# A gated-delta-rule inverse on one core: quadrant products and predicated copies in place of masked blocks and subtractions

## The reference, cut to what matters

```python
decay = jnp.exp(jnp.where(incl, G[..., :, None] - G[..., None, :], -jnp.inf))
kb = k * beta[..., None]
L = jnp.where(strict, jnp.einsum('bhncd,bhnsd->bhncs', kb, k) * decay, 0.0)
sol = lax.linalg.triangular_solve(L + jnp.eye(CHUNK), rhs, left_side=True, lower=True)
```

## Time and profile before

| what | value |
|---|---|
| median of 3 runs | 2124.07 us (2120.09 to 2124.46) |
| profiled execution, its own time | 2125.45 us |
| its span | 2123.6 us |
| mean granted TensorE clock | 0.997 |
| TensorE busy | 2078.8 us (98%) |
| VectorE busy | 1498.3 us (71%) |
| ScalarE busy | 891.7 us (42%) |
| GpSimd busy | 178.1 us (8%) |

### The profile page before, as it was taken

The page is one execution under the profiler, slowest core; times in us unless marked ns, Lnnn a source line. Parts: engine busy times, 40 slices in busy tenths (PEclk is TensorE's granted clock), DMA queues, the critical chain, the costliest instruction groups (busy, mean ns, idle before and its releaser), DMA issues.

```text
span 2123.6 us, 35703 instructions
## 1 busy us (share of the span) xinstructions
PE 2078.8 (98%) x14417; PEld 1808.5 (85%) x14417; DVE 1498.3 (71%) x1949; ACT 891.7 (42%) x1174; POOL 178.1 (8%) x152
## 2 busy tenths in 40 slices
PE   8999999999999999999999999999999999999999
PEld 8988888798888798888798878887879998778998
DVE  6968754778745577754697685456688877588887
ACT  3244444334444423444323454445554334664332
POOL 6630000000000000000073300000100000100000
PEclk9999999999999999999999999999999999999999
DMA  8512665552656453655464046565325555414552
GB/s 248 179 42 80 202 195 181 176 183 97 198 179 196 161 179 120 201 195 180 147 188 142 3 149 218 184 190 156 103 68 191 178 188 167 139 50 164 194 178 100
DMA packets 267625, 333.81 MB, mean 157 GB/s; under 512 B 20562, under 2 KB 230613, under 8 KB 267493
## 3 DMA queue, kind: packets, MB, share of 16 engines
q1 hardware_dynamic: 267493, 331.93, 48.3%
HBM read 330.84 MB, written 1.05 MB: 156 GB/s over the span
## 4 chain that ended last, share of the span: by engine, by line
PE 84%; DVE 10%; ACT 3%; issue 2%; SPq 1%; DMA 0%; POOL 0%; DVEq 0%; ACTq 0%
PE bank L586 47%; PE bank L554 25%; DVE pj L2199 2%; PE bank L1065 2%; ACT stat L1590 1%; PE bank L827 1%; PE bank L921 1%; PE bank L991 1%; PE bank L1146 1%; DVE w_hi L2238 1%; PE bank L637 1%; DVE sq L2199 1%; DVE pj L2193 1%; DVE w_lo L2240 1%; DVE pj L2189 1%
## 5 line engine op out<-in xcount | busy, mean ns | idle before, releaser
L2240 DVE TENSOR_TENSOR w_lo<-ring,w_hi 128x2048 fp32r<-128x2048 f32 (+2 forms) x289 | 615.3, 2131 | 371.8 <-ACT w_hi L1635 369.4
L1635 ACT ACTIVATE w_hi<-ring 128x2048 fp32r<-128x2048 f32 (+1 forms) x220 | 418.9, 1905 | 469.0 <-PE bank L586 287.3
L586 PE MATMUL bank<-w_lo,xh 128*128 128x512 f32 x992 | 267.0, 392 | 0.0
L586 PE MATMUL bank<-w_hi,xl 128*128 128x512 f32 x896 | 240.8, 391 | 1.0 <-DVE xl L2189 0.7
L586 PE MATMUL bank<-w_hi,xh 128*128 128x512 f32 x896 | 241.1, 391 | 0.6 <-ACT xh L1590 0.6
L554 PE MATMUL bank<-xh,w_lo 128*128 128x256 f32 (+2 forms) x1832 | 241.7, 284 | 0.0
L554 PE MATMUL bank<-xh,w_hi 128*128 128x256 f32 x1752 | 234.6, 287 | 0.8 <-ACT xh L1590 0.7
L554 PEld LDWEIGHTS bank<-xh,w_lo 128*128 128x128 f32 (+2 forms) x1832 | 228.6, 191 | 1.0
L554 PE MATMUL bank<-xl,w_hi 128*128 128x256 f32 x1752 | 229.3, 284 | 0.0
L554 PEld LDWEIGHTS bank<-xh,w_hi 128*128 128x128 f32 x1752 | 220.2, 191 | 9.6 <-issue 6.7
L554 PEld LDWEIGHTS bank<-xl,w_hi 128*128 128x128 f32 x1752 | 218.0, 191 | 1.0 <-issue 0.7
(11 more groups left out here) (325 smaller groups left out, 2439.1 us busy)
## 6 DMA issues: line engine op xcount, KB each, us to landing
ring<-in_ffn_w_in_dram SPq DMA_DIRECT2D x264, 512.0 KB, 4.5
ring<-in_ffn_w_down_dram SPq DMA_DIRECT2D x88, 512.0 KB, 4.1
ring<-in_gdn_w_in_dram SPq DMA_DIRECT2D x64, 512.0 KB, 5.0
ring<-in_ffn_w_out_dram SPq DMA_DIRECT2D x44, 512.0 KB, 3.7
ring<-in_w_in_dram SPq DMA_DIRECT2D x40, 512.0 KB, 4.7
ring<-in_hgrn_w_in_dram SPq DMA_DIRECT2D x32, 512.0 KB, 4.5
ring<-in_gla_w_in_dram SPq DMA_DIRECT2D x24, 512.0 KB, 4.7
ring<-in_gdn_w_out_dram SPq DMA_DIRECT2D x16, 512.0 KB, 4.4
```

Of the source, the lines that this page charges most:

```text
L586: m = nc.tensor.matmul(bank[:, 0:width], xin[:, k0 + k, rows_of], w[:, k, c * width:(c + 1) * width], start=(first and step == 0 and k == ...
L1635: nc.scalar.activation(taken(high_part(u), u), taken(ring[:, u % RING, :], u), ACT.Copy).then_inc(*act_hi.tick())
L2240: v.tensor_tensor(w_lo[:, u % RING, 0:share], w[:, 0:share], high[:, 0:share], ALU.subtract).then_inc(*dve_lo.tick())
```

## The change

`crossed` names the two off-diagonal quadrants. The stationary matrix of the product is now a whole 128x128 tile per matrix, `lb`, that holds minus the two diagonal blocks of L, each in the other block's columns, and zero elsewhere. One product of 128x128 by 64 columns serves both blocks; it does so by putting each block's result in the other block's partitions. X and XT of a matrix therefore lie in opposite halves. L isn't masked for levels 1 to 4; what must not change is left out when the result is put in place, by a predicated copy through a level mask instead of a subtraction. For level 5 GpSimd masks `lb` once. The order of the TensorE instructions changes to product of group n, correction of group n-2. The masks need a transposed form, made once in layer 0 by four transpositions and two copies.

```diff
-        lb_masked, lb = (flat(ct)[:, ...] for n in range(2))
+        crossed = ((blocks[0], blocks[1]), (blocks[1], blocks[0]))
+        lb = ct
...
+                    if layer == 0 and n == N_CONV - 2:
+                        masks_transposed()
...
+            def masks_transposed():
+                b = psum.claim(pe, "level masks")
+                pe.wait_ge(*pool_setup.at("constants"))
+                for lv in range(1, 5):
+                    m = nc.tensor.transpose(b[:, (lv - 1) * P:lv * P], level_mask(lv), ident[:, :])
...
+                gdn_product(layer, 1, GROUPS[0])
+                gdn_product(layer, 1, GROUPS[1])
+                gdn_correct(layer, 1, GROUPS[0])
+                gdn_transpose(layer, GROUPS[2])
+                gdn_correct(layer, 1, GROUPS[1])
+                gdn_transpose(layer, GROUPS[3])
+                gdn_product(layer, 1, GROUPS[2])
+                gdn_product(layer, 1, GROUPS[3])
+                for lv in range(2, 7):
                     for n, g in enumerate(GROUPS):
-                        (product of level lv, group g; then correction of the group before)
+                        gdn_product(layer, lv, g)
+                        gdn_correct(layer, lv if n > 1 else lv - 1, GROUPS[n - 2])
+                gdn_correct(layer, 6, GROUPS[2])
+                gdn_correct(layer, 6, GROUPS[3])
...
+            def gdn_product(layer, lv, g):
+                (level 6: as before, one 64x64 product a matrix)
-                                for r in blocks:
-                                    m = nc.tensor.matmul(b[r, cols_of], lb_masked[r, j, :], inverse(j)[r, :], start=True, stop=True)
+                    m = nc.tensor.matmul(b[:, of], lb[:, j, :], inverse(j), start=True, stop=True)
...
             def gdn_correct(layer, lv, g):
+                if lv < 6:
+                    bt = psum.claim(pe, "zt", layer, lv, g)
+                if lv > 1:
+                    pe.wait_ge(*dve_gdn.at("XT", layer, lv - 1, g))
-                    for left, right, c in ((transposed(j), cx[:, j, :], c), (cx[:, j, :], transposed(j), c + T)):
-                        for r in blocks:
-                            m = nc.tensor.matmul(b[r, c:c + HALF2], left[r, :], right[r, :], start=True, stop=True)
+                    for r, to in crossed:
+                        if lv < 5 or to == blocks[0]:
+                            nc.tensor.matmul(b[to, of], transposed(j)[r, :], cx[r, j, :], start=True, stop=True)
+                        m = nc.tensor.matmul(bt[r, of], cx[r, j, :], transposed(j)[r, :], start=True, stop=True)
...
 (GpSimd)
+                g.memset(lb[:, :, :], 0.0).then_inc(*pool_gdn.tick("beside", layer))
                 g.memset(inv[:, 16:32, 0:HALF2], 0.0).then_inc(*pool_gdn.tick("cleared", layer))
-                (24 masked copies of 128x256, six for each group)
+                for q in GROUPS:
+                    g.tensor_copy(xx[:, q, 1, :, :], (identity, broadcast))
+                for q in GROUPS:
+                    pool.wait_ge(*pe_gdn.at("cx", layer, 4, q))
+                    last = lb[:, 4 * q:4 * q + 4, :].rearrange("p h (two n) -> p (h two) n", two=2)
+                    g.tensor_tensor(last, last, level64[:, 5:6, :].to_broadcast([P, 8, HALF2]), ALU.mult)
...
 (VectorE)
+                def put(sig_key, to, which, mask, values):
+                    m = halves(mask.bitcast(U32), sig_key[1], which)
+                    to, values = halves(to, sig_key[1], which), halves(values, sig_key[1], which)
+                    v.copy_predicated(to, m.to_broadcast(list(to.shape)), values)
                 def first_inverse(g):
-                    tt(s, xx[:, g, 1, :, :], (identity), lb_masked[:, 4 * g:4 * g + 4, :], ALU.subtract, "XT", layer, 0, g)
+                    for r, to in crossed:
+                        put(("XT", 0, g), xx[to, g, 1, :, :], 1, level64[r, 0:1, :], lb[r, 4 * g:4 * g + 4, to])
                     if lv < 5:
-                        tt(s, X, X, b[:, :], ALU.subtract, "X", layer, lv, g)
+                        put(("X", lv, g), xx[:, g, 0, :, :], 0, level64_t[:, lv - 1:lv, :], by_head(b))
+                        put(("XT", lv, g), xx[:, g, 1, :, :], 1, level64[:, lv:lv + 1, :], by_head(bt))
-                    if lv == 4:
-                        last_gates()
+                        if lv == 4 and g in GROUPS[1::2]:
+                            last_gates(GROUPS.index(g) // 2)
```

More of the change, by code:

```diff
@@ L267, in build @@
         later = sb("later", [P, P])
-        level = sb("level", [P, 7, P])
+        level = sb("level", [P, WHOLE_BLOCKS, P])
         level64 = sb("level64", [P, 6, HALF2])
+        level64_t = sb("level64_t", [P, 4, HALF2])
         ident64 = sb("ident64", [P, HALF2])
@@ L378, in halves, with level_mask @@
             return ap.rearrange("p h (n two c) -> p h n two c", two=2, c=1 << lv)[:, :, :, which, :]
+        def level_mask(lv):
+            return level[:, lv, :] if lv < WHOLE_BLOCKS else dec[:, lv - WHOLE_BLOCKS, 0:P]
         def par(col):
@@ L1044, in gdn_transpose @@
                 for j in range(4 * g, 4 * g + 4):
-                    for r in blocks:
-                        m = nc.tensor.matmul(b[r, (j % 4) * HALF2:(j % 4 + 1) * HALF2], transposed(j)[r, :], ident[r, r],
+                    for r, to in crossed:
+                        m = nc.tensor.matmul(b[to, (j % 4) * HALF2:(j % 4 + 1) * HALF2], transposed(j)[r, :], ident[r, r],
                                              start=True, stop=True)
                 m.then_inc(*pe_gdn.tick("transposed", layer, g))
+            def gdn_product(layer, lv, g):
+                b = psum.claim(pe, "cx", layer, lv, g)
+                pe.wait_ge(*(act_gdn.at("X", layer, g) if lv == 1 else dve_gdn.at("X", layer, lv - 1, g)))
+                if lv == 1:
+                    pe.wait_ge(*act_gdn.at("blocks", layer, g))
+                if lv == 5:
+                    pe.wait_ge(*pool_gdn.at("masked", layer, g))
+                for j in range(4 * g, 4 * g + 4):
+                    of = slice((j % 4) * HALF2, (j % 4 + 1) * HALF2)
+                    if lv == 6:
+                        t0 = (j // 8) * T
+                        m = nc.tensor.matmul(b[HALF2:HALF, of], lt[0:HALF2, j % 8, t0 + HALF2:t0 + HALF], inverse(j)[0:HALF2, :],
+                                             start=True, stop=True)
+                        continue
+                    m = nc.tensor.matmul(b[:, of], lb[:, j, :], inverse(j), start=True, stop=True)
+                m.then_inc(*pe_gdn.tick("cx", layer, lv, g))
@@ L1536, in _ @@
             keep(rot96[:, 80:96], [[-1, 16]], -64, 1, op=ALU.not_equal, fill_=1.0)
-            for lv in range(7):
+            for lv in range(6):
                 h = 1 << lv
-                m = level[:, lv, :].rearrange("p (n a c) -> p n a c", a=2, c=h)
+                m = level_mask(lv).rearrange("p (n a c) -> p n a c", a=2, c=h)
                 fill(m[:, :, 0, :], 0.0)
@@ L1972, in diagonal_blocks @@
                     act.wait_ge(*dve_gdn.at("lt", layer, h0 + 3))
-                    for r in blocks:
-                        run(s, lb[r, 4 * g:4 * g + 4, :], lt[r, h0:h0 + 4, t0 + r.start:t0 + r.stop], ACT.Copy, "blocks", layer, g)
+                    act.wait_ge(*pool_gdn.at("beside", layer))
+                    for r, to in crossed:
+                        run(s, lb[r, 4 * g:4 * g + 4, to], lt[r, h0:h0 + 4, t0 + r.start:t0 + r.stop], ACT.Copy, "blocks", layer, g,
+                            scale=-1.0)
                 for h in range(8):
@@ L2319, in project @@
                         dve.wait_ge(*act_setup.at("params", 2))
+                    if layer == 0 and n == N_CONV - 1:
+                        masks_transposed()
                     dve.wait_ge(*pe_unit.at("unit", layer, n))
```

78 lines of the change are left out of this document (32 added, 46 removed).

## The result

The changed kernel took 2129.38 us (median of 8 runs, 2124.71 to 2134.78), the kernel before beside it 2119.8 (8 runs, 2118.64 to 2124.46): ratio 1.004, 95% interval 1.003 to 1.005. Timed again beside before (7 runs and 19) it took 2127.19 against 2121.7: 1.0035, 1.0024 to 1.0047. The forecast was 2129.5 and 0.25% slower; by the medians the change costs 0.35 to 0.4%.

A forecast was written before the change was run, and what follows sets the result against it. The stage was taken as bound by TensorE. Terms summed to +2.4 us a stage, +4.8 for two, plus 0.6 in layer 0: +5.4, giving 2129.5 us, 0.25% slower, range 2122 to 2145.

The forecast's parts named there:

- Part 1: Products of levels 1 to 5: 128-column weight loads 0.111 us apart, 0.89 us a group instead of 0.47; +8.4 us a stage.
- Part 2: Switches between 128x128 products and 64x64 corrections: 17 stretches a stage at 0.33 us each, +5.5 us.
- Part 3: Corrections of levels 1 to 5 on four quadrants at once: 0.47 us a group instead of 0.93, -9.3 us a stage.
- Part 4: Instruction order, per stage: level ends -1.0 us, level 1 -0.9 (0 to -1.9), level 6 -0.3 (-0.9 to +0.9).
- Part 5: Other engines: VectorE's copies and GpSimd's masks change nothing in the stage; extra VectorE copies in layer 0 add +0.6 us.
- Quadrants taking turns: Rival: only two quadrants work at a time, corrections give back 0.9 of 9.3 us a stage; 2146.3 us, chance 0.17.
- Free change of form: Rival: switching array form costs nothing or is nearly hidden; 2118.5 us, chance 0.13 together with fast loads.
- Fast wide loads: Rival: wide weights don't set the product's pace, 0.05 us less per record; 2113 us, chance 0.13 together with free form change.
- Waits absorbing it: Rival: levels 1 and 6 lose their pauses whole and VectorE's extra layer 0 work hides; about 2126 us, chance 0.10.

The follow-up runs named there:

- halves: Changed kernel with each 128x128 product made as two products of 128 rows by 64 columns; one run, 2122.07 us.
- wide_moving: Changed kernel with 128 moving columns instead of 64 in the 128x128 products, half of them wanted; one run, 2129.77 us.
- paired: Changed kernel with the order product, product, correction, correction at levels 2 to 5, halving the changes of form; one run, 2124.51 us.
- one_put: Changed kernel without one of VectorE's two predicated copies of the first inverse in groups 1 and 3; one run, 2126.69 us.
- masks_pool: Changed kernel with the transposed masks built by GpSimd at setup instead of by TensorE transpositions and VectorE copies; one run, 2125.35 us.
- quad_twice: quad_products with each transposed correction of levels 2 to 5 issued twice, 512 TensorE records more; one run, 2134.14 us.
- quad_products: Changed kernel with each 128x128 product of levels 1 to 5 made as two 64x64 products on off-diagonal quadrants; 2121.01 us (12 runs), ratio 1.0003 to before.
- quad_narrow: quad_products with 32 moving columns instead of 64 in products and corrections of levels 2 to 5; one run, 2138.07 us.

## Why the prediction was right

**Part 1, wide product, +8.4: right.** Loads 0.111 apart; halves and wide_moving confirm that the load's 128 columns, not the moving side, cost the time.

**Part 2, change of form, +5.5: the cause is right, its sum with the rest too.** The group time came out at 1.66 as forecast. The gaps are in the trace as forecast: the last quadrant record starts at 171.51 and the first wide load at 171.66, the last wide record at 172.49 and the first quadrant load at 172.69. paired saved 0.22 a change instead of 0.33, and the remaining 0.11 is its products' wait for VectorE.

**Part 3, four quadrants, -9.3: right.** 0.47 us a group. The Trainium skill's rule (TensorEngine Tiling (Array Packing), section Restrictions and Gotchas), that row tiles can't reach one PSUM bank at the same time, would have made it 2146 us; here z takes results of both row halves in one bank, and its transpose in another, with records of all four quadrants starting at 141.79 to 141.81. The Trainium skill's page TensorE: Matmul & The Clock Gate (section Wait — 56ns, not 53.3ns?) gives some 25 ns as the least distance from start to start. Here 32 records in 0.47 us are 15 ns each across quadrants, so that figure doesn't bound them; within one quadrant the starts are 0.058 us apart. In both places the measurement decides.

**Part 4, order: right at the level ends, wrong at level 1 and level 6.** The level ends have no pause (-1.0 as forecast). Level 1 gave 0.1 and not 0.9: VectorE's copies of 0.44 to 0.49 hold the last transposition; one_put, with one fewer, gave 0.45 back in layer 3. Level 6 cost +0.85 and not -0.3: VectorE's three operations a group, 0.42 each, queue up ahead of the last products (173.44 to 176.55). The price lay inside the bounds given; I had taken the better end. Together this is +2.0 us a stage. The working for level 6: from the end of level 5's last product to u0 pass 5.27 us in before, with two corrections of 0.93 still in it, and 5.73 in after, with three of 0.47, so 3.4 against 4.3, less the rest of a change of form that Part 2 has.

**What the prediction did not have: supply.** The earlier trace rows shows "145.82 0.39 issue" in before, and I passed over it. Gaps of that kind between two matmul starts are 0.61 and 0.27 us in layer 0 of before, and 0.75 and 0.64 in layer 3; less 0.03 each, 0.8 and 1.3 us. All four end 1.2 to 1.6 us after a packet of instructions. At 14.6 ns a record before just outruns its supply of 14.8. After has 320 records a level where before has 384, with slow wide ones among them, and shows no such gap in levels 2 to 5. The pauses that before had are gone in it, which the sum should have had as a gain. So 2.4 + 2.0 - 0.8 = 3.6 (measured 3.30) and 2.4 + 2.0 - 1.3 = 3.1 (2.54): two misses of opposite sign, +4.0 and -2.1, partly cancel, and the forecast of +4.8 met 5.8. That they cancel is luck, and 0.3 and 0.6 us stay unexplained.

Luck too is how near the median came, 2129.38 against 2129.5. The forecast started from a profiled execution of 2125.45 us and medians of 2124.07, while before's median beside the change was 2119.8; the first difference of medians was 9.6 us and the second 5.5. What bears the forecast out is the 6.2 us at full clock against 5.4.

**Part 5 and layer 0:** GpSimd and VectorE cost nothing in levels 2 to 5, as forecast. Layer 0's entry is 0.8 us later (forecast 0.6); the chain of waits of after shows it:

```profile
98.84 3.36 DVE pick L2285
...
102.70 0.20 DVE level L2290
102.90 0.14 DVE level L2291
```

L2285 starts 0.68 later than its fellow in the earlier trace rows, behind the two mask copies. masks_pool brought VectorE's part of it back (`pick` at 97.7 us) but, with TensorE late for another reason, not the unit's start; how much of the 0.8 us the copies are is shown only to within the 0.4 us by which executions differ.

**The rivals.** Quadrants taking turns: refuted by the four starts within 0.02 us. Free change of form: refuted by paired, whose pace of two groups falls by 0.22 in spite of a new wait. Fast wide loads: refuted by the 0.111. Waits absorbing it: the level ends gave it all, levels 1 and 6 did not.

## What to carry to other kernels

Halving the number of products with a wider stationary matrix is worth something only if the load isn't what sets the pace: with 64 moving columns a 128-column float32 load costs 0.11 us a record, more than the two 64-column records it replaces (0.058 on two quadrants), and each change from 64x64 to 128x128 and back costs 0.2 to 0.3 us more. Count records against the supply of instructions (here 256 per 3.8 us) before spending effort on parallel quadrants; beyond that, by the reading above, only fewer instructions help, which no run here tried by itself. When a queue of another engine holds several operations a group, look at the last level of a stage, where no further group hides them.

## What the runs showed of the hardware that was not expected

- TensorE's instructions come in lots of 256, one 16 KB packet in the instruction queue each. Where they are used up at 9.6 ns each, 0.9 to 1.5 us of "issue" follow, until 1.2 to 1.65 us after the packet has landed; the average over layer 0 of quad_twice is 14.8 ns an instruction.
- Four 64x64 quadrants run at once, 0.015 us a record, into two banks. Two 128x64 halves run side by side at 0.039.
- The clock stayed at 2.4 GHz in quad_products with TensorE busy for 13.5 of 20 us, and fell to 1.2 in quad_narrow, whose records have half the columns, after 3.2 busy us of 6.
